# Load and first norm of a hybrid decoder step: nine row buffers, small work made between two blocks, another split of the low parts

## The chip, the cores and the metric

One core of one Trainium2 chip runs the whole program. The metric is the device time of one execution in microseconds, as the median of several executions.

## What is computed

One layer of a hybrid decoder, for 1,040 prompt tokens (16 meta tokens and 1,024 new ones) and 32 sample tokens (8 sequences of 4) over a paged cache. The part that the change touches is the beginning:

```python
def rms_norm(x, g):
    x32 = x.astype(jnp.float32)
    r = lax.rsqrt(jnp.mean(x32 * x32, axis=-1, keepdims=True) + NORM_EPS)
    return (x32 * r).astype(x.dtype) * g

def trunk_layer(x, pos, attend, conv_prev, ffn_prev, w_in, w_pa, w_pb, w_o, conv_w,
                norm1, norm2, ffn_up, ffn_conv_w, ffn_down):
    Bn, T, _ = x.shape
    hn = rms_norm(x, norm1)
    proj = hn @ w_in
    ...
    a = attend(q, k, v, qi, ki, wi)
    u, conv_new = causal_dwconv(cc * cx, conv_prev, conv_w)
    b = cb * u
    mixed = jax.nn.sigmoid(ga) * (a @ w_pa) + jax.nn.sigmoid(gb) * (b @ w_pb)
    x = x + mixed @ w_o
    hn2 = rms_norm(x, norm2)
    ...
```

Behind it come the index scores and the choice of 256 keys for each query, sparse attention, the gated short convolution, the output projection and a convolutional feed-forward with 2,816 channels. All is float32.

## The kernel before, in words

All 1,072 tokens are worked on together, features on the partitions: x is held turned, as `xt` (`core.x`), 8 feature blocks by 1,074 columns. Every product of float32 operands is made of three float32r products: high part by high part, low by high and high by low. The high part is ScalarE's copy of the operand to float32r, the low part the operand less its high part, on VectorE or POOL (GpSimd). `split_product` (L229) issues these matmuls: for each of eight feature blocks k, three column parts of 358 by three products, nine matmuls.

The program is a row of stages, each a block with a part for each engine. All engines wait for each other where one stage ends and the next begins; within a stage each engine runs its own list of instructions in the order in which it is written, held by semaphores. There is no planner; the order is the code's. Stages that matter here:

1. `load_stage` (from L295). Nine blocks of token rows, eight of 128 and one of 48, come by DMA from SP's queue into three buffers `x_rows` of 4 KB a partition (L329). Block t+3 is issued when TensorE has turned block t and ScalarE has squared it (waits in L327 and L328). For each block ScalarE sums the squares of each row (L353), TensorE turns it in eight transposes into one of three pairs of PSUM banks (L375), and VectorE copies those into `xt` (L397). When all nine are through, TensorE turns the small tables: conv weights and states (4 transposes, L380), norm gains (8, L383) and feed-forward conv weights and states (22, L386). ScalarE copies them out of PSUM (L356, L358, L360) and scales the constants ident and place (L363, L364). VectorE makes the gather rows, the cache rows that index keys are gathered from, out of the page table (L402 to L409). SP fetches the first three slices of w_in into `w_raw` (L575) and stores xt to `x_save` (L333). ScalarE's queue had issued the small tables, the constants and the page table at the start (L345 to L348).
2. `norm_stage` (from L451). VectorE and ScalarE make the inverse root of each token's mean square (`inverse_roots`, L412 on: ScalarE's `Sqrt` at L418, one Newton step on VectorE, L423 to L430). VectorE makes nine diagonal matrices of them (L504), TensorE multiplies ones by these, which spreads the numbers over the partitions (L481). For each feature block k VectorE makes `norm_y` (L508), ScalarE its high part `act_hi` (L493), and VectorE (odd k) or POOL (even k) its low part `act_lo` (L464). ScalarE and POOL also make the high and low part of the first slices of w_in (`w_hi` L546, `w_lo` L551): POOL's first ahead of its low parts, its second behind them. TensorE makes the first product, with 68 output rows, k by k as the low parts come.
3. `index_stage`. TensorE goes on with two products of 128 output rows, 72 matmuls each, on the same operands, then ropes and scores follow.

The order on POOL in the norm stage is written thus:

```python
            ahead.lo(pool, 0)
            for k in range(0, KB, 2):
                low(pool, k)
            ahead.lo(pool, 1)
```

Of the kernel before, what the change touches and what calls it, by code (L numbers as in the profile page):

```python
# [27 lines left out]
ACT = mybir.ActivationFunctionType  # L28
ALU = mybir.AluOpType
# [265 lines left out]
def load_stage(nc, core, ahead):  # L295
# [4 lines left out]
    rows = [r2(f"x_rows{s}", [128, D]) for s in range(3)]  # L300
# [7 lines left out]
    with ExitStack() as ctx:  # L308
# [3 lines left out]
        x_in = [sem(f"x_in{s}") for s in range(3)]  # L312
# [3 lines left out]
        parts = [len(x_rows(ins, t)) for t in range(NT)]  # L316
        x_count = [16 * sum(parts[t % 3:t + 1:3]) for t in range(NT)]
        ident = core.c["ident"]
        with nc.Block() as block:

            @block.sync
            def _(sp):
                sp.dma_start(core.cbuf[:, 0:128], ins["constants"][:, 0:128]).then_inc(ident_in, 16)
                for t in range(NT):
                    if t >= 3:
                        sp.wait_ge(turned, t - 2)
                        sp.wait_ge(squared, t - 2)  # L327
                    for (a, b), src in x_rows(ins, t):  # L328
                        sp.dma_start(rows[t % 3][a:b, :], src).then_inc(x_in[t % 3], 16)  # L329
# [6 lines left out]
            def _(act):  # L336
# [12 lines left out]
                act.wait_ge(ss_ok, 1)  # L349
                for t in range(NT):  # L350
                    act.wait_ge(x_in[t % 3], x_count[t])
                    after(act, squared, t)
                    act.activation(junk[0:ROWS[t], :], rows[t % 3][0:ROWS[t], :], ACT.Square,  # L353
                                   accum_out=core.ss[0:ROWS[t], t:t + 1]).then_inc(squared, 1)
                act.wait_ge(small_turned, 1)
                act.activation(core.conv[:], core.flat(6, CB * 19).rearrange("p (k r) -> p k r", r=19),  # L356
                               ACT.Copy).then_inc(small_copied, 1)
                act.activation(core.gains[:], core.flat(6, 200)[:, 100:100 + 3 * KB].rearrange("p (k r) -> p k r", r=3),  # L358
                               ACT.Copy).then_inc(small_copied, 1)
                act.activation(core.fconv[:], core.flat(7, FB * 19).rearrange("p (k r) -> p k r", r=19),  # L360
                               ACT.Copy).then_inc(small_copied, 1)
                act.wait_ge(consts_in, 16)
                act.mul(core.identb[:], core.c["ident"], -BIG)  # L363
                act.mul(core.place[:].rearrange("p s r -> p (s r)"), core.c["place"], -BIG)  # L364

            @block.tensor
            def _(pe):
                pe.wait_ge(ident_in, 16)
                for t in range(NT):
                    n = ROWS[t]  # L370
                    pe.wait_ge(x_in[t % 3], x_count[t])
# [79 lines left out]
def norm_stage(nc, core, which, name, ahead, total=None):  # L451
# [15 lines left out]
    with nc.Block() as block:  # L467
# [30 lines left out]
        def _(dve):  # L498
# [3035 lines left out]
```

## Time and profile before

| | |
|---|---|
| median of 3 runs | 1863.91 us |
| the runs | 1863.91, 1855.33, 1866.0 us |
| profiled execution, its own time | 1859.58 us |
| its span in the profile | 1857.8 us |
| granted TensorE clock, mean | 0.965 |
| TensorE busy, matmuls | 1717.0 us, 92% |
| VectorE busy | 1266.9 us, 68% |
| ScalarE busy | 682.3 us, 37% |
| POOL busy | 347.6 us, 19% |
| moved by DMA | 201.28 MB, 108 GB/s over the span |

The span is what the profiler records, first instruction to last; the execution's own time is 1.8 us longer. A timeline row names its start, its length, engine, line, operation, output and inputs, and in brackets how long the engine had been idle and what ended that. Rows of the same kind that follow each other are merged; their length is that of the whole group. "PE" is TensorE's matmuls, "PEld" its weight loads, "ACT" ScalarE, "DVE" VectorE, "ACTq" and "SPq" the queues on which DMAs are issued. The granted clock is a share of 2.4 GHz: 1.00 is 2.4, 0.50 is 1.2 GHz.

### The profile page before, as it was taken

Reading aid. Unit: us, or ns where it says so; the run is one execution under the profiler, and the core shown is the slowest. Engines: PE = TensorE matmul, PEld = TensorE weight load, DVE = VectorE, ACT = ScalarE, POOL = GpSimd, SP = SyncE. Lnnn points to the kernel's source line nnn. Section 1 sums busy time; section 2 is a strip of 40 time slices with the busy share of each in tenths; the row PEclk is TensorE's granted clock in tenths of the full one; section 3 lists DMA queues with packets and bytes.
Section 4 is the critical chain, followed back from the end, with each engine's and each line's share of the span. In section 5 each row is a group of like instructions: output and inputs, shape, how many; then the busy total and the mean of one; then the engine's idle time right before and its main releaser. Section 6 shows DMA issues by size and latency. Waiting matters only on the chain.

```text
span 1857.8 us, 30831 instructions
## 1 busy us (share of the span) xinstructions
PE 1717.0 (92%) x12025; PEld 1619.4 (87%) x12025; DVE 1266.9 (68%) x2316; ACT 682.3 (37%) x1207; POOL 347.6 (19%) x232
## 2 busy tenths in 40 slices
PE   4959999899999869988779989999999999999997
PEld 4834999899999857766569988999999999999997
DVE  4373766788888968967444268777777776664564
ACT  3253011121211245665542145333333333554453
POOL 0544143222222341222326220000000000000000
PEclk7989999999999979999989999999999999999999
DMA  8133211122222031344637312222222222776553
GB/s 263 46 93 93 57 48 39 55 67 93 78 89 64 5 110 53 134 137 136 206 116 259 105 40 88 70 77 86 81 70 73 89 71 89 257 238 201 162 180 114
DMA packets 161878, 201.28 MB, mean 108 GB/s; under 512 B 20057, under 2 KB 123449, under 8 KB 161201
## 3 DMA queue, kind: packets, MB, share of 16 engines
q1 hardware_dynamic: 142884, 125.91, 22.5%
q0 software_dynamic: 13888, 54.02, 8.7%
q10 hardware_dynamic: 4978, 19.59, 2.8%
q8 instruction: 87, 1.43, 0.3%
q14 instruction: 41, 0.34, 0.1%
HBM read 163.27 MB, written 35.61 MB: 107 GB/s over the span
## 4 chain that ended last, share of the span: by engine, by line
PE 53%; DVE 4%; ACT 3%; issue 2%; DMA 1%; POOL 0%; DVEq 0%; ACTq 0%
PE ps L2303 23%; PE ps L2708 13%; PE ps L229 7%; PE ps L1894 3%; PE ps L1938 2%; PE ps L1876 2%; PE ps L1860 1%; PE ps L1949 1%; PE ps L1975 1%; DMA down_raw<-in_ffn_down 1%; ACT probs L2082 0%; PE ps L2696 0%; DVE probs_turned L2160 0%; DVE operand_lo L3172 0%; DVE up_P_lo L3134 0%
## 5 line engine op out<-in xcount | busy, mean ns | idle before, releaser
L229 PE MATMUL ps<-act_hi,w_hi 128*128 128x358 f32 (+1 forms) x1080 | 360.9, 334 | 11.8 <-POOL act_lo L464 5.2
L2303 PE MATMUL ps<-operand_hi,up_P_hi 128*128 128x268 f32 x1232 | 354.4, 288 | 8.9 <-issue 6.8
L229 PE MATMUL ps<-act_lo,w_hi 128*128 128x358 f32 (+1 forms) x1080 | 354.7, 328 | 0.0
L229 PE MATMUL ps<-act_hi,w_lo 128*128 128x358 f32 (+1 forms) x1080 | 353.7, 328 | 0.0
L2303 PE MATMUL ps<-operand_lo,up_P_hi 128*128 128x268 f32 x1232 | 353.4, 287 | 0.0
L2303 PE MATMUL ps<-operand_hi,up_P_lo 128*128 128x268 f32 x1232 | 353.2, 287 | 0.0
L2303 PEld LDWEIGHTS ps<-operand_hi,up_P_hi 128*128 128x128 f32 x1232 | 234.0, 190 | 9.4 <-issue 7.0
L2303 PEld LDWEIGHTS ps<-operand_lo,up_P_hi 128*128 128x128 f32 x1232 | 233.6, 190 | 0.0
L2303 PEld LDWEIGHTS ps<-operand_hi,up_P_lo 128*128 128x128 f32 x1232 | 233.4, 189 | 0.0
L229 PEld LDWEIGHTS ps<-act_hi,w_hi 128*128 128x128 f32 (+1 forms) x1080 | 204.4, 189 | 14.2 <-issue 11.8
L229 PEld LDWEIGHTS ps<-act_lo,w_hi 128*128 128x128 f32 (+1 forms) x1080 | 205.0, 190 | 1.2
L229 PEld LDWEIGHTS ps<-act_hi,w_lo 128*128 128x128 f32 (+1 forms) x1080 | 203.6, 189 | 0.9
L551 POOL TENSOR_TENSOR w_lo<-w_raw,w_hi 128x1024 fp32r<-128x1024 f32 (+1 forms) x57 | 138.1, 2424 | 313.9 <-ACT w_hi L546 302.2
L2708 PE MATMUL ps<-inner_hi,down_hi 128*128 128x384 f32 (+1 forms) x528 | 172.4, 326 | 1.5 <-DVE down_lo L3295 1.5
L2708 PE MATMUL ps<-inner_hi,down_lo 128*128 128x384 f32 (+1 forms) x528 | 171.2, 324 | 0.0
L2708 PE MATMUL ps<-inner_lo,down_hi 128*128 128x384 f32 (+1 forms) x528 | 171.1, 324 | 0.0
L1102 DVE TENSOR_SCALAR_CACHE_REDUCE count_junk<-scores,candidate 128x384 uint8<-128x384 f32 (+1 forms) x186 | 163.6, 943 | 0.0
L3295 DVE TENSOR_TENSOR down_lo<-down_raw,down_hi 128x512 fp32r<-128x512 f32 x132 | 90.5, 690 | 101.4 <-ACT down_hi L2937 100.7
L2937 ACT ACTIVATE down_hi<-down_raw 128x512 fp32r<-128x512 f32 x132 | 82.6, 628 | 109.5 <-DMA down_raw<-in_ffn_down 108.9
L2816 ACT ACTIVATE up_P_hi<-w_sum 128x512 fp32r<-128x512 f32 x88 | 55.5, 632 | 170.3 <-PE ps L2303 161.7
L2708 PEld LDWEIGHTS ps<-inner_hi,down_hi 128*128 128x128 f32 x528 | 99.1, 188 | 2.4 <-DVE down_lo L3295 2.1
L2708 PEld LDWEIGHTS ps<-inner_lo,down_hi 128*128 128x128 f32 x528 | 99.1, 188 | 0.0
(421 smaller groups left out, 3114.9 us busy)
## 6 DMA issues: line engine op xcount, KB each, us to landing
down_raw<-in_ffn_down SPq DMA_DIRECT2D x132, 256.0 KB, 3.0
w_raw<-in_w_in SPq DMA_DIRECT2D x32, 512.0 KB, 3.8
w_raw<-in_ffn_up SPq DMA_DIRECT2D x48, 256.0 KB, 3.4
inner_save<-xt SPq DMA_DIRECT2D x22, 536.0 KB, 2.7
xt<-in_ffn_up SPq DMA_DIRECT2D x40, 256.0 KB, 3.3
inner_raw<-inner_save SPq DMA_DIRECT2D x44, 192.0 KB, 3.8
x_save<-xt SPq DMA_DIRECT2D x1, 4296.0 KB, 13.1
mix_b<-row ACTq DMA_DIRECT2D x8, 537.0 KB, 3.6
```

Source lines behind the costliest of these rows:

```text
L229: last = pe.matmul(core.acc(out_set)[0:rows, c, :], w(k), b(k)[:, c * CH:(c + 1) * CH], start=(i == 0 and n == 0), stop=(i == kblocks - 1 ...
L551: eng.tensor_tensor(self.core.wl[slot][:, 0:width], self.core.wr[slot][:, 0:width], self.core.wh[slot][:, 0:width].bitcast(F32), ALU.subtr ...
L1102: ins = self.dve.tensor_scalar(hd.junk[x % 2][:, 0:part.shape[1]], part, value(i), None, ALU.is_ge, ALU.add, accum_out=hd.count[:, i:i + 1])
L1860: last = pe.transpose(core.flat(4, 512, rows)[:, a:a + n], probs[2 * (s % 2) + v][0:n, 128 * k:128 * k + rows], ident[0:n, 0:n])
L1876: last = pe.matmul(core.flat(first_bank(s, v), NK[qb], n)[:, a:a + width], mine, ks[0][p, a:a + width], start=(x == 0), stop=(x == 2))
L1894: last = pe.matmul(core.flat(5, NKV * n).rearrange("p (v n) -> p v n", v=NKV), a[0:rows, k, :], b[0:rows, k, :, :], start=(k == 0 and x == 0),
L1938: last = pe.transpose(core.flat(6 + b4 % 2, 512)[:, 128 * s:128 * s + 128], got[slot][:, half(r, s)], ident)
L2303: last = pe.matmul(out[:, c, :], w[:, 128 * k:128 * k + 128], b(k)[:, cols], start=(name in OPENING and k == 0 and n == 0), stop=(k == 3 a ...
L2708: last = pe.matmul(core.ps[:, MG * (s % 2) + m, 0:w], a[:, 128 * m:128 * m + 128], c[o % H_SLOTS][:, 0:w], start=(f == 0 and z == 0), stop ...
L2816: act.activation(up_w[name][0][:], src, ACT.Copy).then_inc(w_hi, 1)
L2937: act.activation(d_hi[y][:], d_raw[y][:], ACT.Copy).then_inc(dw_hi, 1)
L3295: dve.tensor_tensor(d_lo[y][:], d_raw[y][:], d_hi[y][:].bitcast(F32), ALU.subtract).then_inc(dw_lo, 1)
```

## The change

In `load_stage`: nine buffers `x_rows`, one for each block, laid where the norm's `act_hi` and `act_lo` will stand; SP issues all of x without a wait. TensorE turns the small tables behind the fourth block (t = 3). VectorE makes the gather rows behind its copy of the fourth block. ScalarE scales ident and place and copies the small tables behind the squares of the fifth block (t = 4). Ahead of its first square it takes the root of one number.

In `norm_stage`: VectorE makes the low parts of k = 0, 2, 4, 6 and 7, POOL those of 1, 3 and 5. POOL first waits for all nine diagonals.

```diff
-    rows = [r2(f"x_rows{s}", [128, D]) for s in range(3)]
+    r1 = At(nc, Map.R1, Map.W)
+    rows = [r1(f"x_rows{t}", [128, D]) for t in range(NT)]
...
                 for t in range(NT):
-                    if t >= 3:
-                        sp.wait_ge(turned, t - 2)
-                        sp.wait_ge(squared, t - 2)
                     for (a, b), src in x_rows(ins, t):
-                        sp.dma_start(rows[t % 3][a:b, :], src).then_inc(x_in[t % 3], 16)
+                        sp.dma_start(rows[t][a:b, :], src).then_inc(x_in[t], 16)
...
                 act.wait_ge(ss_ok, 1)
+                act.wait_ge(zeroed, 1)
+                act.activation(core.root[:, 0:1], core.x[:, 0, TOK:TOK + 1], ACT.Sqrt)
                 for t in range(NT):
...
+                    if t == SMALL + 1:
+                        act.wait_ge(consts_in, 16)
+                        act.mul(core.identb[:], core.c["ident"], -BIG)
+                        act.mul(core.place[:].rearrange("p s r -> p (s r)"), core.c["place"], -BIG)
+                        act.wait_ge(small_turned, 1)
...
                     last.then_inc(turned, 1)
...
+                    if t == SMALL:
+                        turn_small()
...
                     dve.tensor_copy(core.x[:, :, 128 * t:128 * t + ROWS[t]], src[:, :, 0:ROWS[t]]).then_inc(copied, 1)
...
+                    if t == SMALL:
+                        gather_rows()
...
+    BY_DVE, BY_POOL = (0, 2, 4, 6, 7), (1, 3, 5)
...
             for k in range(KB):
                 dve.scalar_tensor_tensor(y[k][:], core.x[:, k, 0:TOK], core.gains[:, k, which:which + 1],
                                          spread_out, ALU.mult, ALU.mult).then_inc(scaled, 1)
-                if k % 2 == 0 and k:
+                if k % 2:
                     low(dve, k - 1)
             low(dve, KB - 1)
...
             pool.memset(core.al[:, :, TOK:TW].bitcast(F32), 0.0)
+            pool.wait_ge(diagonal, NT)
             ahead.lo(pool, 0)
-            for k in range(0, KB, 2):
+            for k in BY_POOL:
                 low(pool, k)
             ahead.lo(pool, 1)
```

`SMALL` is 3. `turn_small` and `gather_rows` hold the same instructions as before.

ScalarE's list from the load stage's first square to the norm's first instruction, before (`squares` is the square's throw-away output, `norm_numbers` holds sums, means and roots; L319 and the branch behind it are the change of stage):

```order
17 L353 ACTIVATE squares,norm_numbers<-x_rows_146 128x1024
18 L353 ACTIVATE squares,norm_numbers<-x_rows_147 48x1024
19 L356 ACTIVATE conv_w_and_states<-ps 128x76
20 L358 ACTIVATE gains<-ps 128x24
21 L360 ACTIVATE ffn_conv_w_and_states<-ps 128x418
22 L363 ACTIVATE ident_bf_55<-constants 128x128
23 L364 ACTIVATE place_bf_54<-constants 128x256
24 L319 UNCONDITIONAL_BRANCH
25 L487 UNCONDITIONAL_BRANCH
26 L418 ACT_TABLE_LOAD
27 L418 ACTIVATE norm_numbers<-norm_numbers 128x9
```

and in the changed kernel:

```order
15 L353 ACTIVATE squares,norm_numbers<-x_rows_149 128x1024
16 L357 ACTIVATE ident_bf_55<-constants 128x128
17 L358 ACTIVATE place_bf_54<-constants 128x256
18 L360 ACTIVATE conv_w_and_states<-ps 128x76
19 L362 ACTIVATE gains<-ps 128x24
20 L364 ACTIVATE ffn_conv_w_and_states<-ps 128x418
21 L353 ACTIVATE squares,norm_numbers<-x_rows_150 128x1024
22 L353 ACTIVATE squares,norm_numbers<-x_rows_151 128x1024
23 L353 ACTIVATE squares,norm_numbers<-x_rows_152 128x1024
24 L353 ACTIVATE squares,norm_numbers<-x_rows_153 48x1024
25 L320 UNCONDITIONAL_BRANCH
26 L501 UNCONDITIONAL_BRANCH
```

Five instructions went from behind the last square to behind the fifth, and the table load ahead of the norm's root is gone.

VectorE's list in the norm stage, from the first y on, before:

```order
17 L508 SCALAR_TENSOR_TENSOR norm_y_402<-xt,gains,ps 128x1072
18 L508 SCALAR_TENSOR_TENSOR norm_y_403<-xt,gains,ps 128x1072
19 L508 SCALAR_TENSOR_TENSOR norm_y_404<-xt,gains,ps 128x1072
20 L464 TENSOR_TENSOR act_lo<-norm_y_403,act_hi 128x1072
21 L508 SCALAR_TENSOR_TENSOR norm_y_405<-xt,gains,ps 128x1072
22 L508 SCALAR_TENSOR_TENSOR norm_y_406<-xt,gains,ps 128x1072
23 L464 TENSOR_TENSOR act_lo<-norm_y_405,act_hi 128x1072
```

and in the changed kernel, where `norm_y_398` is the first:

```order
18 L522 SCALAR_TENSOR_TENSOR norm_y_398<-xt,gains,ps 128x1072
19 L522 SCALAR_TENSOR_TENSOR norm_y_399<-xt,gains,ps 128x1072
20 L472 TENSOR_TENSOR act_lo<-norm_y_398,act_hi 128x1072
21 L522 SCALAR_TENSOR_TENSOR norm_y_400<-xt,gains,ps 128x1072
22 L522 SCALAR_TENSOR_TENSOR norm_y_401<-xt,gains,ps 128x1072
23 L472 TENSOR_TENSOR act_lo<-norm_y_400,act_hi 128x1072
```

The first low part now stands behind the second y and is VectorE's.

POOL's list in the changed kernel's norm stage:

```order
9 L566 TENSOR_TENSOR w_lo_68<-w_raw_62,w_hi_65 128x544
10 L472 TENSOR_TENSOR act_lo<-norm_y_399,act_hi 128x1072
11 L472 TENSOR_TENSOR act_lo<-norm_y_401,act_hi 128x1072
12 L472 TENSOR_TENSOR act_lo<-norm_y_403,act_hi 128x1072
13 L566 TENSOR_TENSOR w_lo_69<-w_raw_63,w_hi_66 128x1024
```

Before, four low parts stood there (k = 0, 2, 4, 6); now three (k = 1, 3, 5).

## Rows read from the trace of the kernel before

**Rows 1.** The page: the span, and each engine's busy time
```profile
span 1857.8 us, 30831 instructions
...
PE 1717.0 (92%) x12025; PEld 1619.4 (87%) x12025; DVE 1266.9 (68%) x2316; ACT 682.3 (37%) x1207; POOL 347.6 (19%) x232
```

**Rows 2.** Busy time by stretch: length, engines, then granted clock, DMA share, GB/s
```profile
16.00:18.00 2.00, 1.51 (x7) 1.51 (x8) 1.21 (x1) 1.40 (x3) 0.00 (x0) 1.00 0.43 113
...
22.00:24.00 2.00, 1.09 (x8) 0.86 (x8) 0.26 (x1) 1.14 (x2) 0.00 (x0) 1.00 0.93 294
...
26.00:28.00 2.00, 2.00 (x13) 1.67 (x12) 0.48 (x1) 1.91 (x4) 0.00 (x0) 0.50 1.23 278
...
52.00:54.00 2.00, 2.00 (x10) 1.62 (x9) 2.00 (x2) 1.35 (x2) 1.40 (x1) 0.72 0.00 0
...
54.00:56.00 2.00, 2.00 (x15) 1.68 (x14) 2.00 (x2) 2.00 (x3) 1.14 (x1) 1.00 0.00 0
...
62.50:86.50 24.00, 23.95 (x146) 23.76 (x146) 0.00 (x0) 3.20 (x4) 6.55 (x3) 1.00 0.32 79
```

**Rows 3.** Timeline of the load stage: start us, us, engine, line, operation
```profile
16.49 3.17 PE L375 MATMUL ps<-constants,x_rows 128*128 128x128 f32 x16 [0.55 <-DMA x_rows<-in_x_prompt]
...
19.90 1.10 PE L375 MATMUL ps<-constants,x_rows 128*128 128x128 f32 x8 [0.24 <-DMA x_rows<-in_x_prompt]
...
26.86 1.06 ACT L353 ACTIVATE squares<-x_rows 48x1024 f32<-48x1024 f32 x1
...
27.52 1.69 DVE L397 COPY xt<-ps 128x1024 f32<-128x1024 f32 x2 [2.28 <-PE ps L375]
...
29.73 2.51 PE L386 MATMUL ps<-constants,ffn_conv_rows 19*128 19x19 f32 x22
32.28 0.23 ACT L356 ACTIVATE conv_w_and_states<-ps 128x76 f32<-128x76 f32 x1 [4.26 <-PE ps L386]
...
33.08 0.43 ACT L364 ACTIVATE place_bf<-constants 128x256 bf16<-128x256 f32 x1
```

**Rows 4.** DMA issues of 0 to 60 us: median us from issue to landing
```profile
x_rows<-in_x_prompt SPq DMA_DIRECT2D x7, 512.0 KB, 5.3
constants<-in_constants ACTq DMA_DIRECT2D x1, 1561.0 KB, 11.6
...
pages<-in_page_table ACTq DMA_DIRECT2D x1, 128.0 KB, 12.8
```

**Rows 5.** Timeline of the norm stage up to the spreading products
```profile
33.76 1.28 ACT L418 ACT_TABLE_LOAD   x1 [0.26 <-PEq L319]
...
35.90 1.33 POOL L551 TENSOR_TENSOR w_lo<-w_raw,w_hi 128x544 fp32r<-128x544 f32 x1 [1.98 <-ACT w_hi L546]
35.95 1.29 DVE L430 SCALAR_TENSOR_TENSOR norm_numbers<-norm_numbers 128x9 f32<-128x9 f32 x1
37.28 1.85 DVE L504 TENSOR_SCALAR norm_diagonals<-constants,norm_numbers 128x128 f32<-128x128 f32 x9
...
37.62 4.37 PE L481 MATMUL ps<-norm_diagonals,constants 128*128 128x128 f32 x18 [5.38 <-DVE norm_diagonals L504]
```

**Rows 6.** Timeline from the first y to the next stage's first matmul
```profile
42.03 3.81 DVE L508 SCALAR_TENSOR_TENSOR norm_y<-xt,gains,ps 128x1072 f32<-128x1072 f32 x3 [2.90 <-PE ps L481]
...
44.56 5.99 POOL L464 TENSOR_TENSOR act_lo<-norm_y,act_hi 128x1072 fp32r<-128x1072 f32 x2 [7.34 <-ACT act_hi L493]
45.76 2.45 DVE L464 TENSOR_TENSOR act_lo<-norm_y,act_hi 128x1072 fp32r<-128x1072 f32 x1
...
47.22 0.54 PE L229 MATMUL ps<-act_hi,w_hi 128*68 128x358 f32 x1 [5.23 <-POOL act_lo L464]
...
58.68 1.28 DVE L464 TENSOR_TENSOR act_lo<-norm_y,act_hi 128x1072 fp32r<-128x1072 f32 x1 [1.17 <-ACT act_hi L493]
...
58.76 3.44 POOL L551 TENSOR_TENSOR w_lo<-w_raw,w_hi 128x1024 fp32r<-128x1024 f32 x1
...
62.55 0.41 PE L229 MATMUL ps<-act_hi,w_hi 128*128 128x358 f32 x1 [0.54 <-PEq L467]
```

More of the change, by code:

```diff
@@ L315, in load_stage @@
         ins = core.i
-        parts = [len(x_rows(ins, t)) for t in range(NT)]
-        x_count = [16 * sum(parts[t % 3:t + 1:3]) for t in range(NT)]
+        x_count = [16 * len(x_rows(ins, t)) for t in range(NT)]
+        SMALL = 3
         ident = core.c["ident"]
@@ L360, in _ @@
[L360 to L364, printed above, removed]
+                    if t == SMALL + 1:
[3 more added lines that the diff above has]
+                        act.wait_ge(small_turned, 1)
+                        act.activation(core.conv[:], core.flat(6, CB * 19).rearrange("p (k r) -> p k r", r=19),
+                                       ACT.Copy).then_inc(small_copied, 1)
+                        act.activation(core.gains[:], core.flat(6, 200)[:, 100:100 + 3 * KB].rearrange("p (k r) -> p k r", r=3),
+                                       ACT.Copy).then_inc(small_copied, 1)
+                        act.activation(core.fconv[:], core.flat(7, FB * 19).rearrange("p (k r) -> p k r", r=19),
+                                       ACT.Copy).then_inc(small_copied, 1)
@@ L393, in _, with gather_rows @@
                 dve.memset(core.x[:, :, TOK:TW], 0.0).then_inc(zeroed, 1)
+                def gather_rows():
+                    dve.wait_ge(pages_in, 16)
+                    dve.wait_ge(consts_in, 16)
+                    dve.tensor_tensor(picked[:].rearrange("p (m q) -> p m q", q=PPG),
+                                      pages[:].rearrange("p (m q) -> p m q", q=PPG),
+                                      core.c["page"].rearrange("p (m q) -> p m q", m=1).broadcast_to([128, NB * NGA, PPG]),
+                                      ALU.mult).then_inc(own, 1)
+                    dve.wait_ge(own, 1)
+                    dve.tensor_reduce(page[:], picked[:].rearrange("p (m q) -> p m q", q=PPG), AX.X, ALU.add).then_inc(own, 1)
+                    dve.wait_ge(own, 2)
+                    dve.tensor_scalar(core.rows[:], page[:], float(PAGE // RUN), core.c["lane"], ALU.mult, ALU.add)
                 for t in range(NT):
@@ L464, in low, with lows @@
         eng.tensor_tensor(core.al[:, k, 0:TOK], y[k][:], core.ah[:, k, 0:TOK].bitcast(F32), ALU.subtract)\
-            .then_inc(lo_odd if k % 2 else lo_even, 1)
+            .then_inc(lo_p if k in BY_POOL else lo_d, 1)
+    def lows(pe, k):
+        if k in BY_POOL:
+            pe.wait_ge(lo_p, BY_POOL.index(k) + 1)
+        else:
+            pe.wait_ge(lo_d, BY_DVE.index(k) + 1)
     with nc.Block() as block:
@@ L484, in _ @@
             ahead.w.product(pe, 0, 0, 0, m=ahead.m,
-                            before=lambda k: pe.wait_ge(lo_odd if k % 2 else lo_even, k // 2 + 1)).then_inc(ahead.ready, 1)
+                            before=lambda k: lows(pe, k)).then_inc(ahead.ready, 1)
         @block.scalar
```

50 lines of the change are left out of this document (18 added, 32 removed).

## The prediction

> **What bounds the kernel now.** I read the page first, for the shares; then busy time and granted clock in short stretches of the first 90 us, where the change lies; then the timeline there, engine by engine; last the DMA issues. TensorE is busy for 1717 of 1857.8 us [rows 1], so after its first long product the kernel hangs on that engine, and a block of time taken out ahead of that product moves all that follows, unchanged, by as much. That only holds because nothing later waits for something that doesn't move along: x_save, the weights and the gathers are issued on signals of the same stages.
>
> In the first 90 us it is different. From 62.5 to 86.5 us TensorE is busy 23.95 of 24 us [rows 2]. Before that it isn't the bound. The load stage hands over at 33.76 us, where ScalarE starts on the norm [rows 5]. Read backwards: the last thing ended there is ScalarE's copy for place (33.08 and 0.43), which follows the three small copies from 32.28 us on, and these idled 4.26 us for TensorE's small transposes, 34 of them, the last 22 in 2.51 us [rows 3], 0.114 us each. So the tail is: x copied at 29.21 (27.52 and 1.69), ScalarE's last square done at 28.02, and yet 4.5 us pass until the stage ends.
>
> The norm then goes in a chain: table for the root 1.28, root, four small steps on VectorE of which the last took 1.29 instead of about 0.17, nine diagonals 1.85, nine spreading products 4.37 [rows 5]. The first y starts at 42.03. From there VectorE, ScalarE and POOL share the rows; the first product starts at 47.22 and the next stage's first at 62.55 [rows 6], which is 20.52 us behind the first y.
>
> **The load stage.** Small transposes, three copies, two scalings and the gather rows are moved from behind the ninth block to behind the fourth or fifth. Nothing is added there but one root of one number, done while ScalarE would wait for x in any case.
>
> The transfers: three buffers made x late. In 16 to 18 us the DMA engines were busy 0.43 of the time with 113 GB/s, in 22 to 24 us 0.93 at 294 GB/s [rows 2], so some 316 GB/s were there for x alone. Left after about 16.5 us are blocks 5 to 8, 3 x 512 KB and 192 KB, 1.77 MB: 5.6 us at that rate, so the last lands at about 22.5 us instead of 26.8. Constants and page table need 11.6 and 12.8 us to land [rows 4], so at 15.6 and 17.3; the deeper SP queue was never empty before 16 us anyway, so I leave both where they are. The weights come behind x on the same queue, 1.33 MB, at some 27 us, and are wanted later.
>
> TensorE: the fourth and fifth block took 3.17 us from 16.49 on, 1.58 each; the sixth 1.10 [rows 3]. The small ones therefore start at 18.1. At the old 0.114 us they end at 22.0; the sixth block's pace, 0.7 of its forerunners', would make it 20.8; between the two I take 21.5. Then VectorE copies blocks 4 to 8: it needs 1.25 a block and 0.55 for the last (1.69 for a whole and a short one, with their overlap), so if TensorE turns a block in 1.10, copies run from 22.6 to 28.2. If it turns one in 1.58 throughout, from 22.0: 4 x 1.58 and about 1.0 for the short block, then the short copy, 29.9. ScalarE: five squares by 19.0, scalings 0.75, waits for the small transposes, copies 0.75, then four squares at 1.25: done at 27.5 to 28. Gather rows, 1.1 us, fill VectorE's wait for the fifth block. With x_save's issue of 0.35 and the hand-over (0.25 behind ScalarE's last end in rows 3 and 5) the stage ends at 28.8 or 30.5, and I take 29.1, nearer to the first since the sixth block's pace held already at 19.9 us. **Gain 4.7 us**, 3.3 to 5.4.
>
> **Ahead of y.** The table load of 1.28 at 33.76 goes, for the Sqrt table, loaded in front, serves Square and Copy too: there is no second load in the instruction order. VectorE's last small step ran 35.95 to 37.24 and POOL's w_lo 35.90 to 37.23 [rows 5]: it stood still until POOL ended. POOL now waits for all nine diagonals, so 1.12 us go. What is queued behind POOL's new wait is w_lo and its first low part; the diagonals end about 3.2 us into the stage, w_lo (1.33) at 4.6, and the product wants it at 10. Gain 2.4; less 0.2 for semaphores, **2.2 us**.
> The Trainium skill (ScalarE: Activation LUTs, What ACT_TABLE_LOAD costs) prices a switch of sets at 1283 ns for the load plus 1380 ns of drain, 2.66 us in all; this trace agrees with the first only, since the root started 1.29 us after its load. By the page the sum would be 1.4 us better.
>
> **The low parts.** One takes VectorE 1.28 (58.68) and POOL 2.4 (two of them 5.99, less 1.28 in which VectorE went between). The two stand in each other's way: VectorE's low part of 45.76 took 2.45, ending 1.28 after POOL's first had ended, and POOL's w_lo of 58.76 took 3.44 beside VectorE's [rows 6]. The y steps read one operand from PSUM and don't wait. With these rules I laid out the new order, in us from the first y. VectorE: y0, y1, low 0 at 2.5, y2, y3, low 2 at 6.3, y4, y5, low 4 at 10.1, y6, y7 until 13.85, low 6, low 7. POOL: low 1 at 3.8, low 3 at 7.6, low 5 at 11.4 until 13.85, w_lo. Here low 6 and w_lo want the same port at once, and whoever comes second waits; in either order, with POOL's w_lo at 2.4, low 7 ends at about 18.9. TensorE starts at 3.9 instead of 5.2, but is held at low 7 and has nine matmuls left, 9 x 0.166 [rows 2]: end 20.4, hand-over 20.8 against 20.52. **Loss 0.3 us**, from a gain of 1.3 (were only the early start to count) to a loss of 1.5.
> The Trainium skill (SBUF — State Buffer, Who interferes with whom) says that a VectorE instruction with two SBUF inputs and a POOL instruction that reads SBUF exclude each other for a whole instruction, the first issued winning. The rows of 45.76 and 58.76 agree. If VectorE could go on beside POOL, the new order would end low 7 at 16.4, TensorE would be held by nothing but its own 14.8 us, and the sum be 1.7 us better.
>
> **Sum.** 4.7 + 2.2 - 0.3 = 6.6 us. Against the profiled execution, 1859.58, that is 1853.0. The runs shown are 1855.33, 1863.91 and 1866.0; the profiled one lies 4.3 under their median. The mean of all four is 1861.2, and 6.6 off it gives **1854.6**, my forecast. About 0.5%, 9.3 us, is what a measurement of this kernel tells from no change, so the likeliest result is no change that can be told, on the faster side.
>
> **Rivals.**
> (a) The deeper queue brings x no sooner: the last block still lands at 26.8. For it: in the first 16 us the DMA engines were full in any case, and transfers of 512 KB took 5.3 us each [rows 4]. Against: the idle share at 16 to 18 us. Copies then end at 29.2 as now, and with the small work out of the tail the stage ends at 29.8: gain 4.0 + 2.2 - 0.3 = 5.9, 1855.3. Chance 0.15.
> (b) The clock is at 2.4 GHz where it was at 1.2. The granted clock was 0.50 from about 26 to 53 us [rows 2], over the spreading products and the first third of the first product. TensorE now has fewer rests between 16 and 28 us. If the nine spreading products take half of 4.37, y starts 2.2 us sooner, and transposes at the better pace save another 0.6: gain 9.4, and 1851.8. Against: it worked without rest from 25.6 to 32.2 us and stayed at 0.50. Chance 0.2.
> (c) VectorE and POOL collide more often than laid out, by one POOL low part, 2.4 us: low 4 and low 6 each come within 0.1 us of a POOL instruction. Gain 4.2, 1857.0. Chance 0.1.
> (d) **Slower.** The hold at low 6 or low 7, up to 1.8 us, and the hand-over right behind it let the clock fall to 1.2 GHz, and the next stage's 144 matmuls run at about 0.30 us instead of 0.166 (in the first product 5.9 us at half clock went for some 19). It decides from 6.6 / 0.134 = 49 matmuls on; with all 144 the change costs 19.3 - 6.6 = 12.7 us, 1873.9. For it: once at 0.50, the clock stayed there for 27 us. Against: before, TensorE rested 2.1 us ahead of 22.9 and the clock was still 1.00 in 22 to 24. Chance 0.05.
> The Trainium skill (TensorE: Matmul & The Clock Gate, Why this matters for your kernels) has the rests between bursts of matmuls throw the engine back to the half rate, which is the mechanism of (d); no row here shows it at a rest as short as 1.8 us.
>
> **Numbers.** Forecast 0.5, (a) 0.15, (b) 0.2, (c) 0.1, (d) 0.05. All but (d) lie between gains of 4.2 and 9.4; the four runs of before scatter by 4 to 5 us around their mean, and their medians by less. So 1847.5 to 1861.0 leaves out (d) and the ends of the scatter. Faster by over 0.5%: most of (b), three in ten of the forecast, a little of (a), together 0.33; slower 0.05 for (d); 0.62 between.
>
> **What would show it.** The norm's first instruction at 28.5 to 30.8 us instead of 33.76; squares without a table load between root and load; the diagonals starting 1.4 us into the norm instead of 3.5; y0 6.1 us into it; the next stage's first matmul 20.8 us behind y0, with a hold of 1 to 2 us ahead of the seventh or eighth row; x landed by 23 us. The prediction is wrong if the stage still ends beyond 31 us, if the clock is under 1.00 after 60 us where it wasn't, or if the time between the index stage's first matmul and the end isn't the same 1795 us within 3.

## The result, and the profile after

| | kernel before | changed kernel |
|---|---|---|
| median of 20 runs each | 1863.74 us | 1856.38 us |
| range of the runs | 1855.33 to 1868.98 | 1851.46 to 1861.92 |
| ratio of the times | 1 | 0.9969 [0.9961, 0.9978] |

The medians lie 7.4 us apart; the ratio says 5.8 us less (4.1 to 7.3): within 0.5%, on the faster side. The forecast was 1854.6, 6.6 us less. Below stand the same four points of the two profiled executions. "Forecast" is the gain that the prediction gave to the step.

| us from the span's start | before | changed | gain of the step | forecast |
|---|---|---|---|---|
| the norm's first instruction | 33.76 | 30.69 | 3.07 | 4.7 |
| first y | 42.03, 8.27 later | 36.41, 5.72 later | 2.55 | 2.2 |
| next stage's first matmul | 62.55, 20.52 later | 56.66, 20.25 later | 0.27 | -0.3 |
| end of the span | 1795.3 later | 1797.8 later | -2.5 | 0 |

The first three steps give 5.89 us and the last takes 2.5 back, so the spans differ by 3.4. The 2.5 isn't to be read as a price of the change: the profiled execution of the kernel before, 1859.58, lies 4.2 us under that kernel's median, the changed one's, 1856.2, at its own. TensorE's busy time is what it was [rows 1], as the page of the changed kernel shows.

```profile
span 1854.4 us, 30826 instructions
...
PE 1719.0 (93%) x12025; PEld 1620.5 (87%) x12025; DVE 1267.3 (68%) x2317; ACT 681.3 (37%) x1207; POOL 340.9 (18%) x231
```

**The load stage.** The timeline of the changed kernel's load stage (start us, us, engine, line, operation, idle before):

```profile
7.14 16.19 SPq L590 DMA_DIRECT2D w_raw<-in_w_in  x3
...
14.29 1.09 PE L389 MATMUL ps<-constants,x_rows 128*128 128x128 f32 x8 [2.49 <-DMA x_rows<-in_x_prompt]
...
16.60 1.97 PE L389 MATMUL ps<-constants,x_rows 128*128 128x128 f32 x8 [1.22 <-DMA x_rows<-in_x_prompt]
...
19.80 2.51 PE L378 MATMUL ps<-constants,ffn_conv_rows 19*128 19x19 f32 x22
...
22.24 6.08 PE L389 MATMUL ps<-constants,x_rows 128*128 128x128 f32 x40
...
25.95 3.95 DVE L414 COPY xt<-ps 128x1024 f32<-128x1024 f32 x4 [0.48 <-PE ps L389]
...
29.93 0.35 SPq L331 DMA_DIRECT2D x_save<-xt  x1
30.69 0.11 POOL L530 MEMSET act_hi<- 128x16 f32 x1 [30.23 <-POOLq L320]
```

Here TensorE never waits for x again after 16.60: the fourth block, the small transposes from 18.50 and the last five blocks follow on each other to 28.3, and the copies end at 29.90 behind them. All the small work stands in that unbroken chain. Two paces can be told apart: transposes of a whole block start 0.11 us apart at the quick one and 0.21 at the slow one, the small ones 0.06 and 0.11. Busy time of the same kernel by stretch (length, engines, then granted clock, DMA share, GB/s) and one row of its DMA issues (the last is the time from issue to landing in us) say what the transfers and the clock did:

```profile
16.00:18.00 2.00, 1.40 (x7) 1.40 (x8) 0.65 (x1) 1.19 (x3) 0.00 (x0) 0.50 1.04 412
...
20.00:22.00 2.00, 2.00 (x21) 2.00 (x21) 0.82 (x3) 0.00 (x0) 0.00 (x0) 0.50 1.17 214
22.00:24.00 2.00, 2.00 (x11) 1.96 (x11) 0.00 (x0) 1.65 (x5) 0.00 (x0) 0.50 1.27 233
24.00:26.00 2.00, 2.00 (x11) 2.00 (x11) 1.27 (x2) 1.82 (x5) 0.00 (x0) 0.54 1.21 289
26.00:28.00 2.00, 2.00 (x22) 1.83 (x21) 2.00 (x2) 1.74 (x4) 0.00 (x0) 1.00 0.44 108
...
x_rows<-in_x_sample SPq DMA_DIRECT2D x1, 128.0 KB, 17.3
```

The transfers ran at 412 GB/s in 16 to 18 us where 113 stood before [rows 2], but only at 214 and 233 in 20 to 24 us, and constants and page table had their part of it. The last piece of x, issued at 6.68, landed 17.3 us later, at 24.0. The kernel before had it at 26.4; my forecast was about 22.5. The rate was as forecast: from the landing of the fourth block at 16.6 on, five blocks, 2.29 MB, came in 7.4 us, 310 GB/s against my 316. But I had taken the fifth block as landed by then, and ScalarE waited for it until 17.96. Nothing hung on that: TensorE came to the last block at 27.6. But the clock was at its lower level, 1.2 GHz, from about 16 to 26 us. In 24 to 26 us TensorE does 11 transposes in 2 us, in 26 to 28 us, at 2.4 GHz, 22 (six of them of the last, short block).

**Ahead of y, and the low parts.** The same timeline from the norm's start:

```profile
30.94 0.21 ACT L425 ACTIVATE norm_numbers<-norm_numbers 128x9 f32<-128x9 f32 x1 [3.11 <-DVE norm_numbers L428]
...
31.83 0.17 DVE L437 SCALAR_TENSOR_TENSOR norm_numbers<-norm_numbers 128x9 f32<-128x9 f32 x1
32.03 1.85 DVE L518 TENSOR_SCALAR norm_diagonals<-constants,norm_numbers 128x128 f32<-128x128 f32 x9
32.38 3.99 PE L495 MATMUL ps<-norm_diagonals,constants 128*128 128x128 f32 x18 [4.06 <-DVE norm_diagonals L518]
33.97 1.33 POOL L566 TENSOR_TENSOR w_lo<-w_raw,w_hi 128x544 fp32r<-128x544 f32 x1 [3.12 <-DVE norm_diagonals L518]
...
40.32 0.54 PE L229 MATMUL ps<-act_hi,w_hi 128*68 128x358 f32 x1 [3.95 <-DVE act_lo L472]
...
43.87 2.08 POOL L472 TENSOR_TENSOR act_lo<-norm_y,act_hi 128x1072 fp32r<-128x1072 f32 x1 [1.60 <-ACT act_hi L507]
...
49.61 2.40 POOL L566 TENSOR_TENSOR w_lo<-w_raw,w_hi 128x1024 fp32r<-128x1024 f32 x1
...
49.95 4.37 DVE L472 TENSOR_TENSOR act_lo<-norm_y,act_hi 128x1072 fp32r<-128x1072 f32 x2
...
53.20 0.38 PE L229 MATMUL ps<-act_hi,w_hi 128*68 128x358 f32 x1 [1.15 <-DVE act_lo L472]
```

No table is loaded, the last small step takes 0.17 instead of 1.29 [rows 5], the diagonals start 1.34 us into the norm instead of 3.52, and w_lo follows them. In the low parts, POOL's (k = 1, 3, 5) take 2.08 to 2.10 each. Before, the two with VectorE's between them took 5.99 [rows 6], and the two that met no low part of VectorE took 2.54 and 2.51, so it isn't VectorE alone that made them longer:

```profile
56.29 2.51 POOL L464 TENSOR_TENSOR act_lo<-norm_y,act_hi 128x1072 fp32r<-128x1072 f32 x1 [1.15 <-ACT act_hi L493]
```

That row is of the kernel before, k = 6; VectorE made its last y until 57.51 and then stood idle to 58.68. Whether it is the even k, or what the other engines do beside it in the old split, that makes 2.5 us of 2.1 stays open.

The last two low parts of VectorE take 4.37 together beside POOL's w_lo. TensorE is held for the first of them: 1.15 us ahead of the seventh row (k = 6), with the 18 matmuls of the last two rows still to come, 0.163 us apart. For low 7, which ends at 54.32, 17.9 behind the first y, it isn't held.

### The profile page after: what moved, and what is told of

Its sections match the earlier page's. It is cut to its first block, busy times and chain, and to the rows that moved or that the text cites. A ratio compares the mean times of both kernels' runs of the same rounds, so it can differ in the third digit from the quotient of the medians.

```text
span 1854.4 us, 30826 instructions
## 1 busy us (share of the span) xinstructions
PE 1719.0 (93%) x12025; PEld 1620.5 (87%) x12025; DVE 1267.3 (68%) x2317; ACT 681.3 (37%) x1207; POOL 340.9 (18%) x231
## 4 chain that ended last, share of the span: by engine, by line
PE 53%; DVE 4%; ACT 3%; issue 2%; DMA 1%; POOL 0%; DVEq 0%; ACTq 0%
PE ps L2318 23%; PE ps L2723 13%; PE ps L229 7%; PE ps L1909 3%; PE ps L1953 2%; PE ps L1891 2%; PE ps L1875 1%; PE ps L1964 1%; PE ps L1990 1%; DMA down_raw<-in_ffn_down 1%; ACT probs L2097 0%; PE ps L2711 0%; DVE probs_turned L2175 0%; DVE operand_lo L3187 0%; DVE up_P_lo L3149 0%
```

## Experiments

Theory A is the one that I held when I wrote the expectation, B its rival. "Rest" is the time from the next stage's first matmul to the end of the span. All edits are against the changed kernel.

**1. Is it the buffers or the place of the small work?** Nine buffers, the small work back behind the last block (this, the same for VectorE's gather rows, and `t == SMALL + 1` on ScalarE likewise):

```
-                    if t == SMALL:
+                    if t == NT - 1:
```

> The changed kernel with its nine buffers, but the small transposes, their copies, the scalings and the gather rows stand behind the ninth block again. Theory A (from the fourth block on TensorE never rests, so its sum of work sets the end wherever the small transposes stand, and only the tail behind them differs): TensorE's last small transpose ends at about 28.5 us, ScalarE's three copies 0.75 later, and the norm starts at 29.5 us, about 1.2 us before the changed kernel's 30.69. Theory B (it is taking the small work out of the tail that gave the 3 us, as the prediction had it for most of its 4.7): the norm starts 2.5 to 4 us later than 30.69, at 33.2 to 34.7 us. What follows the norm's start keeps its 5.7 us to the first y and 25.9 us to the next stage's first matmul within 0.5, in both.

Measured, median of nine executions: 1853.68 us (1851.36 to 1860.01), ratio 0.9951 [0.9935, 0.9966]. The norm starts at 27.75, against 30.69 with the small work mid-load. The timeline of TensorE:

```profile
16.31 5.64 PE L389 MATMUL ps<-constants,x_rows 128*128 128x128 f32 x32 [0.23 <-DMA x_rows<-in_x_prompt]
...
22.71 1.80 PE L389 MATMUL ps<-constants,x_rows 128*128 128x128 f32 x16 [0.75 <-DMA x_rows<-in_x_prompt]
...
25.20 1.51 PE L378 MATMUL ps<-constants,ffn_conv_rows 19*128 19x19 f32 x22
```

Theory A is right that the norm comes no later; it comes sooner by more than A said (29.5). The last two blocks wait for x, so x is the bound to 22.7, and the small transposes take 1.51 where they took 2.51. Against 33.76 the stage comes 6.0 us sooner without the new place. About 0.5 of that is the order on ScalarE: the two scalings stand ahead of its wait for the small transposes here, and stood behind the small copies before (to 33.51). Part is the clock: the transposes turn quick at 20.3 here, and stay so over all the small work, so this run alone doesn't settle how much. The times don't settle it either, since the intervals of the two ratios, [0.9935, 0.9966] and [0.9961, 0.9978], meet.

**2. The place without the buffers.** Three buffers with their waits on SP as before, the small work mid-load.

```
-    rows = [r1(f"x_rows{t}", [128, D]) for t in range(NT)]
+    rows = [r1(f"x_rows{t}", [128, D]) for t in range(3)] * 3
...
+                    if t >= 3:
+                        sp.wait_ge(turned, t - 2)
+                        sp.wait_ge(squared, t - 2)
```

> The changed kernel with three row buffers again and SP's waits for them; the small work stays behind the fourth block. Theory A (the nine buffers let x land before TensorE wants it, and three would now be worse than before since each fetch waits for a turned block that stands behind 3.7 us of small transposes): the last blocks land at 28 to 30 us and the norm starts at 32 to 34 us. Theory B (rival (a) of the prediction: the DMA engines were full anyway and the buffers brought nothing): the norm starts within 0.7 us of the changed kernel's 30.69.

Measured, a single execution: 1855.44 us; norm 31.43, between the two ranges. The timeline shows the last two blocks waiting for x:

```profile
21.76 4.72 PE L393 MATMUL ps<-constants,x_rows 128*128 128x128 f32 x24
...
27.39 1.09 PE L393 MATMUL ps<-constants,x_rows 128*128 128x128 f32 x8 [0.91 <-DMA x_rows<-in_x_prompt]
...
29.36 0.69 PE L393 MATMUL ps<-constants,x_rows 48*128 48x48 f32 x8 [0.89 <-DMA x_rows<-in_x_sample]
```

With three buffers x is the bound to the last block; with nine it is TensorE. Beside the changed kernel's 30.69 the buffers' worth is small, 0.74 us. And against 33.76 the small work's place alone is worth 2.3 us, as long as there are three buffers. All of these are single profiles.

**3. The old split of the low parts**, with the wait for the diagonals kept.

```
-    BY_DVE, BY_POOL = (0, 2, 4, 6, 7), (1, 3, 5)
+    BY_DVE, BY_POOL = (1, 3, 5, 7), (0, 2, 4, 6)
```

> The changed kernel with the old split of the low parts (POOL k = 0, 2, 4, 6, VectorE 1, 3, 5, 7), the wait for the diagonals kept. Norm start 30.7 and first y 36.4 us unchanged. Theory A (the new split starts the product 1.3 us sooner and gives it back at the collision of low 6 with POOL's w_lo): next stage's first matmul 20.3 to 20.8 us behind the first y, against 20.25 in the changed kernel. Theory B (the early start is what counts): 21.5 us or more behind the first y.

Measured, a single execution: 1860.84 us. The next stage's first matmul comes 20.48 behind the first y, as before the change (20.52), against 20.25. The timeline has the old collisions again:

```profile
39.51 5.98 POOL L472 TENSOR_TENSOR act_lo<-norm_y,act_hi 128x1072 fp32r<-128x1072 f32 x2 [4.02 <-ACT act_hi L507]
40.71 2.42 DVE L472 TENSOR_TENSOR act_lo<-norm_y,act_hi 128x1072 fp32r<-128x1072 f32 x1
```

The split is worth 0.23 us, a gain where I had a loss of 0.3. The time of 1860.84 says little about it, since the rest took 1801.6 here.

**4. Without POOL's wait for the diagonals** (the line `pool.wait_ge(diagonal, NT)` taken out).

> The changed kernel without POOL's wait for the nine diagonals. Theory A (POOL's w_lo holds the port that VectorE's small steps and diagonals want): one of VectorE's small steps or the diagonals stands still until w_lo, 1.33 us, ends, and the first y comes 0.8 to 1.4 us later than 5.72 us behind the norm's start. Theory B (with the table load gone, the chain on VectorE is ahead of w_lo and they don't meet, or the spreading products hide it): the first y stays within 0.2 us.

Measured, a single execution: 1853.56 us. The timeline around the small steps:

```profile
29.01 1.32 POOL L565 TENSOR_TENSOR w_lo<-w_raw,w_hi 128x544 fp32r<-128x544 f32 x1 [0.93 <-ACT w_hi L560]
29.07 1.29 DVE L437 SCALAR_TENSOR_TENSOR norm_numbers<-norm_numbers 128x9 f32<-128x9 f32 x1
30.40 1.85 DVE L518 TENSOR_SCALAR norm_diagonals<-constants,norm_numbers 128x128 f32<-128x128 f32 x9
```

VectorE stands still until POOL ends, 1.29 instead of 0.17, and the diagonals start 2.48 into the norm instead of 1.34. The 1.12 us of the forecast are right: it is 1.14. The Trainium skill (SBUF — State Buffer, Who interferes with whom) says that a VectorE instruction with two inputs in SBUF and a POOL instruction that reads SBUF exclude each other for a whole instruction; this run agrees, with 1.29 against 0.17.

The load stage held a surprise. Its code is that of the changed kernel to the letter, but the norm starts at 27.92, not 30.69:

```profile
16.05 1.59 PE L389 MATMUL ps<-constants,x_rows 128*128 128x128 f32 x8 [0.53 <-DMA x_rows<-in_x_prompt]
...
18.33 1.52 PE L378 MATMUL ps<-constants,ffn_conv_rows 19*128 19x19 f32 x22
19.78 6.00 PE L389 MATMUL ps<-constants,x_rows 128*128 128x128 f32 x40
```

The small transposes take 1.52 instead of 2.51 and the last five blocks start 2.46 us sooner, 0.55 of it since x came sooner. The other 1.9 us are TensorE's pace. In the changed kernel's profile it had the quick one at the third block (14.29, 1.09) and had lost it by 16 us; here it has it from the fourth block to about 20.5, over just the small work.

**5. POOL's last w_lo behind VectorE's last low part.**

```
+            pool.wait_ge(lo_d, len(BY_DVE))
```

> The changed kernel, but POOL's second w_lo waits until VectorE has made all five of its low parts. Theory A (low 6 and low 7 stood still for w_lo, and that hold set the end of the first product): low 6 and low 7 take 2.5 us together instead of 4.37, the hold ahead of the seventh row goes, and the next stage's first matmul comes 18.7 to 19.3 us behind the first y instead of 20.25; w_lo ends before TensorE does. Theory B (the hold is covered, or w_lo, now last, holds the next stage up instead): 20.0 us or more behind the first y.

Measured, median of nine executions: 1854.9 us (1851.12 to 1860.37), ratio 0.9953 [0.9936, 0.997]. The next stage's first matmul comes 18.87 behind the first y, 1.38 less. The timeline:

```profile
50.78 0.38 PE L229 MATMUL ps<-act_hi,w_hi 128*68 128x358 f32 x1 [0.34 <-POOL act_lo L472]
...
51.03 2.52 DVE L472 TENSOR_TENSOR act_lo<-norm_y,act_hi 128x1072 fp32r<-128x1072 f32 x2
...
53.63 2.38 POOL L567 TENSOR_TENSOR w_lo<-w_raw,w_hi 128x1024 fp32r<-128x1024 f32 x1 [2.91 <-DVE act_lo L472]
```

The pair of low parts goes from 4.37 to 2.52, and the hold of 1.15 ahead of the seventh row is gone; what is left is 0.34 ahead of the sixth, for POOL's low part. So that collision was the price of the new split. One part of theory A fails: w_lo doesn't end before TensorE does. The first product ends at 55.51, w_lo at 56.01, and the next stage starts behind w_lo, so of the 1.9 us that the product gains 0.5 go again.

**6. The small work behind the second block** instead of the fourth.

```
-                    if t == SMALL:
+                    if t == 1:
```

> The changed kernel with TensorE's 34 small transposes behind the second block of x instead of the fourth; ScalarE's and VectorE's work stays where it is. Theory A (behind the second block TensorE waits 2.5 us for x anyway, behind the fourth it has no rest, so the small work is only free there): x blocks 4 to 8 are turned without a gap from about 18 us at full clock or 20 at half, and the norm starts 1 to 2.5 us earlier than the same kernel would at the same clock, that is 26.5 to 29 us. Theory B (only the sum of work counts, or the small tables land too late for this place): the norm starts at 27.9 (full clock) to 30.7 us (half clock), as it did in two runs of this load stage.

Measured, median of four executions: 1852.79 us (1851.11 to 1857.1), ratio 0.9936 [0.9915, 0.9957]. The norm starts at 27.11. The timeline, and the clock of one stretch of it:

```profile
12.90 2.51 PE L378 MATMUL ps<-constants,ffn_conv_rows 19*128 19x19 f32 x22
15.34 6.80 PE L389 MATMUL ps<-constants,x_rows 128*128 128x128 f32 x40
...
22.82 1.71 PE L389 MATMUL ps<-constants,x_rows 128*128 128x128 f32 x16 [0.67 <-DMA x_rows<-in_x_prompt]
...
13.00:14.00 1.00, 1.00 (x12) 1.00 (x11) 0.00 (x0) 0.14 (x1) 0.00 (x0) 1.00 1.08 448
```

The small ones go at the slow pace here too, and it costs nothing: they fill the time in which TensorE waited for the third block anyway (2.49 us at 14.29 in the changed kernel), and the last two blocks wait for x again. Its ratio's interval lies clear of the changed kernel's [0.9961, 0.9978]. The window's clock reads 1.00 at the slow pace. So ahead of its first fall the clock column doesn't tell the pace; durations do. In the kernel before it is the same: the column has 1.00 at 16 to 18 us [rows 2], and the blocks of 16.49 were turned at the slow pace until 18.9.

**7. Without the root ahead of the load** (its two lines on ScalarE taken out).

> The changed kernel without the root of one number ahead of the squares. Theory A (the table load then stands ahead of the norm's root again, 1.28 us on the path, while nothing is added in the load stage): the first y comes 1.0 to 1.3 us later behind the norm's start, 6.7 to 7.4 us instead of 5.7 to 6.1. Theory B (the page's account of a switch, with its drain): 2.4 us or more later.

Measured, a single execution: 1858.15 us. The timeline:

```profile
30.57 1.28 ACT L423 ACT_TABLE_LOAD   x1 [3.43 <-PEq L320]
31.86 0.21 ACT L423 ACTIVATE norm_numbers<-norm_numbers 128x9 f32<-128x9 f32 x1
```

The diagonals start 2.39 into the norm instead of 1.34: the load is worth 1.05 us, since 0.25 of it lies where the root waited for VectorE's first step. The Trainium skill (ScalarE: Activation LUTs, What ACT_TABLE_LOAD costs) puts 1380 ns of drain on top of the load. The measurement decides against that on this path: the root starts 1.29 after its load starts. ScalarE had been idle for 3.43 us ahead of the load, so what a load costs right behind running work isn't shown.

**8. Does work for TensorE between the first blocks keep the clock up?** Nine products of the identity ahead of the first block and eight ahead of the third, into a part of PSUM that is free.

```
+                    for _ in range({0: 9, 2: 8}.get(t, 0)):
+                        pe.matmul(core.flat(7, 128), ident, ident, start=True, stop=True)
```

> The changed kernel with TensorE multiplying ident by ident into a bank not yet in use, nine times ahead of the first block of x and eight times behind the second, where it waits for x anyway (this adds work that no output needs). Theory A (what the load stage lost against my forecast is the clock at 1.2 GHz in the small transposes and blocks 3 to 7, and a busier TensorE gets the higher level): the granted clock is 1.00 between 12 and 24 us, the last 22 small transposes take about 1.5 us instead of 2.51, and the norm starts at 27 to 28 us. Theory B (the clock falls in this stretch all the same, or the fillers push the blocks back): small transposes at 2.5 us and a norm start of 30 us or more.

Measured, a single execution: 1857.09 us; norm 29.93, just under theory B's 30.

```profile
10.35 1.09 PE L391 MATMUL ps<-constants,x_rows 128*128 128x128 f32 x8 [0.96 <-DMA x_rows<-in_x_prompt]
...
18.88 2.46 PE L378 MATMUL ps<-constants,ffn_conv_rows 19*128 19x19 f32 x22
21.27 6.52 PE L391 MATMUL ps<-constants,x_rows 128*128 128x128 f32 x40
...
51.94 0.38 PE L229 MATMUL ps<-act_hi,w_hi 128*68 128x358 f32 x1 [1.80 <-DVE act_lo L474]
...
54.00:55.00 1.00, 1.00 (x5) 0.75 (x4) 0.00 (x0) 0.00 (x0) 0.00 (x0) 0.50 0.00 0
```

The quick pace came earlier, at the second block, but was gone in the small work all the same; the clock was 0.50 from 20 to 24 us. The fillers left rests of 1.38 and 1.40 us ahead of the third and fourth block, so a TensorE without rests wasn't tried.

Further on something came that no other run has. The next stage's first matmul came 21.81 behind the first y, 1.56 later than in the changed kernel. TensorE was held for 1.80 us ahead of the seventh row; at 53.1 us the clock fell to 0.50, and eleven of the last matmuls started 0.30 apart instead of 0.163. That is the mechanism of rival (d), at a smaller price, since the clock was back with the next stage. A hold alone doesn't do it: holds of 1.76 to 1.79 at the same place left the clock at 1.00 in experiments 1, 2 and 6. What fell together here wasn't found.

**9 to 11. The changed kernel once more, and two mixtures**, on one chip with the same executions of the kernel before (median 1861.87 us of 18). `both` is experiments 5 and 6 together, `last_and_w_lo` 1 and 5.

> The changed kernel once more, as the measure for the two beside it on the same chip. The norm starts at 27.9 to 31.4 us, by the clock in the load stage; the next stage's first matmul comes 25.9 us behind that; the time is 0.9955 to 0.998 of the kernel before.

> The changed kernel with both edits that gained on their own: small transposes behind the second block of x, and POOL's second w_lo behind VectorE's last low part. Theory A (the two gains lie in different stages on the same path and add): the norm starts at 26.5 to 29 us, the next stage's first matmul 24.6 us behind it, so 51 to 54 us, and the time is 2 to 4.5 us under that of the changed kernel beside it. Theory B (what follows, with its clock at 1.2 GHz here and there between 100 and 155 us, gives the gain back): the next stage's first matmul as said, but the time within 1 us of the changed kernel's.

> The changed kernel with its nine buffers, the small work behind the ninth block, as before, and POOL's second w_lo behind VectorE's last low part. Theory A (moving the small work from the end to behind the fourth block brought nothing): norm start 27.8 us at full clock to 29.5 at half, next stage's first matmul 24.6 us behind it, and 1 to 3 us less time than the changed kernel beside it. Theory B (the small work's place is worth its 3 to 4 us, and the one run that said otherwise owed it to the clock): norm start at 31 us or more in a profile at half clock, and the time no better than the changed kernel's.

| | median us | ratio | norm's first | behind first y | rest |
|---|---|---|---|---|---|
| changed_again | 1857.58 | 0.9973 [0.9962, 0.9985] | 29.70 | 20.28 | 1800.7 |
| last_and_w_lo | 1852.64 | 0.9949 [0.9931, 0.9967] | 29.14 | 18.87 | 1796.7 |
| both | 1849.34 | 0.9935 [0.9916, 0.9955] | 26.67 | 18.88 | 1795.3 |

The medians are of 12, 7 and 6 executions, and "behind first y" is the next stage's first matmul. `both` beats both kernels: its median lies 12.5 us under the kernel before and 8.2 under the changed one. I had expected 2 to 4.5 under the changed one, and for `last_and_w_lo` 1 to 3 where 4.9 came. In the profiles the early start explains 4.0 and 1.5 of these; the remainder lies in the rest and has no explanation here. The next stage of `both` starts at 51.65, 10.9 us sooner than before. The last wait ahead of it is that of experiment 5, for the w_lo that was put last:

```profile
48.91 2.38 POOL L567 TENSOR_TENSOR w_lo<-w_raw,w_hi 128x1024 fp32r<-128x1024 f32 x1 [2.89 <-DVE act_lo L472]
...
51.65 0.41 PE L229 MATMUL ps<-act_hi,w_hi 128*128 128x358 f32 x1 [0.84 <-PEq L481]
```

**What the load profiles say together.** With nine buffers and the small work mid-load, six profiles have the norm's first instruction at 27.92, 29.70, 30.57, 30.69, 30.87 and 31.39: mean 30.2. With the small work last there are 27.75 and 29.14, with it behind the second block 26.67 and 27.11. So against 33.76 the whole change gives about 3.6 us in this stage (2.4 to 5.8), nine buffers with the small work left last 4.6 to 6.0, the early place 6.7 to 7.1, and the changed kernel's place with three buffers 2.3. The 33.76 is one profile too, and its own scatter isn't known.

**The rest of the span.** It took 1795.3 us before, 1797.8 in the changed kernel's profile and 1800.7 in its second one, with the same instructions; over the other ten kernels 1795.3 to 1801.8, in no order that follows the edits. The busy time of 670 to 930 us, of before, changed_again and both:

```profile
670.00:930.00 260.00, 215.32 (x1952) 167.25 (x1954) 189.28 (x395) 147.94 (x326) 67.75 (x68) 0.94 0.41 136
```
```profile
670.00:930.00 260.00, 217.34 (x1966) 170.50 (x1966) 184.58 (x393) 147.15 (x326) 63.17 (x65) 0.92 0.41 136
```
```profile
670.00:930.00 260.00, 220.07 (x2066) 172.02 (x2067) 184.46 (x400) 151.47 (x343) 63.17 (x65) 0.94 0.41 136
```

The executions with the longest rests, 1800.5 to 1801.8, have 0.91 or 0.92 here (changed_again, small_early, u_small_last, u_old_split), the two with 1795.3 have 0.94, and those between 0.93, the changed kernel's profile too. Two hundredths of the mean are 260 x 0.02 / 0.5 = 10 us more at half clock, which could account for up to 5 us. Rest and clock go together over all thirteen profiles; but no run changed the clock alone, so it isn't shown as the cause. What lets the clock fall in one execution and not in another wasn't found, and whether an earlier start of the stages makes it likelier stays open: `both` starts earliest and has the shortest rest.

## Why the prediction was right, and where it wasn't

**Time and likeliest case: right.** 1856.38 against 1854.6, inside the range, within 0.5% on the faster side. But the sizes were off, and luck had its part: the load stage gave 1.6 us less than forecast, the other two steps 0.9 more. The 0.5% that I took for what can be told from no change was too coarse; the interval of 20 executions each leaves 1 out by far.

**The load stage, 4.7 us: mis-sized.** It measured 3.07, under the lower bound of 3.3, and 3.6 as the mean of six profiles. The step that failed is the choice between two paces: "if TensorE turns a block in 1.10" the copies end at 28.2, "if it turns one in 1.58 throughout" at 29.9, and I took 29.1 for the norm since the sixth block's pace held at 19.9 us. They ended at 29.90: the slow branch. In the kernel before the quick pace lay over 19.0 to 25.8 us, in the changed one over 14.3 to 15.6 and from 25.8 on, and I carried it over to a stage that the change itself had rearranged. (The hand-over took 0.79 where I had 0.60.) The chain was right in kind: small transposes from 18.1, here 18.50, then five blocks without a wait for x. What I never worked out is the same stage with nine buffers and the small work left last. I took the gain for that of the shorter tail, for 4.0 of the 4.7 by rival (a)'s sum; experiment 2 has 2.3 for it, with three buffers. And with x landing sooner TensorE had little left to wait for behind the fourth block, 0.75 us in experiment 1 and 1.45 in `last_and_w_lo`, so that the work put there made its own chain longer. The free place is behind the second block, where the wait remains (experiment 6). That x landed 1.5 us later than forecast, a block short in my sum, had no effect.

**Ahead of y, 2.2 us: right.** Experiments 7 and 4 give 1.05 for the table and 1.14 for the standing still, 2.19 in sum. The profile's 2.55 has 0.38 more from nine spreading products that took 3.99 instead of 4.37; in changed kernels with 4.37 the first y comes 6.10 behind, a gain of 2.17.

**The low parts, -0.3: wrong sign, and the last step wrong.** +0.27 in the profile, 0.23 in experiment 3. TensorE starts 3.91 behind the first y, as said (3.9); low 6 and w_lo collide, as said. But I had TensorE "held at low 7" with nine matmuls left, and it was held at low 6 with eighteen left: low 6 ended at 53.1, and 18 x 0.163 behind it make the product's end, while low 7 was through before its row came. Low 7 ended 17.9 behind the first y and not 18.9. POOL's low part, 2.4 by my division of two collided ones, took 2.1 in the new split; w_lo ended 15.6 behind the first y and not 16.3, and low 7 2.3 behind that. Experiment 5 shows the collision's own price, 1.38, net of the 0.5 that w_lo then costs.

**The rivals.** (a) fell: the last of x landed at 24.0, 2.4 us sooner than before. (b) happened in part, and by the execution: experiment 4 had the quick pace over the small work and gained 2.8 more. (c) didn't happen, POOL's low parts stayed at 2.08 to 2.10. (d) didn't come in the changed kernel: a hold of 1.15 left the clock at 1.00, with products 0.163 us apart behind it. But it isn't impossible: in experiment 8 the clock fell behind a hold of 1.80, for 1.6 us and not 19.

Of the signs that I had named, x missed: it had landed by 24.0 us and not by 23.

**"The same 1795 us within 3": held once, failed once.** 1797.8 in the first profile, 1800.7 in the second. The 1795 was the rest of one execution, and one of the shorter: at the median time of 1863.74 and the same start it would be some 4 us more. So the change needn't have lengthened anything. It fits that 6.9 us of earlier start (62.55 to 55.62) came to 4.3 in the medians of experiment 9 and to 5.8 in the first ratio.

## What to carry to other kernels

Two edits that aim at the same wait aren't to be added up: once the deeper queue had taken the wait for x away, the work moved into it was in the way, and two blocks earlier, in a wait that the queue doesn't touch, it was free. So work out each edit alone as well as all together. Where two engines share a way to memory, look which instruction of the slower engine can go last; a single wait was worth 1.4 us here, a whole new split 0.2. And an expected gain under the scatter of single executions, some 6 us in this kernel, is read at the stage's own instructions in the timeline, not from the end of the span.

## What the runs showed of the hardware that I had not expected

- The same load code took 27.92 to 31.39 us in six executions. The place of TensorE's quick spell differs: over the third block at 14.29 in one, over the small work at 18.33 in another (2.51 and 1.52 us for the same 22 transposes).
- The clock column reads 1.00 from the start until its first fall, even where the transposes have the slow pace (experiment 6).
- POOL's subtraction of 128x1072 took 2.08 to 2.11 us for k = 1, 3 and 5, and 2.49 to 2.54 for the even k of the old split (before, experiment 3) even where VectorE made none beside it. VectorE's took 1.27 or 1.28 for either.
- SP's three issues of the weights took 16.19 us with nine buffers, with nine blocks of x queued ahead of them, and held nobody: x_save was wanted at 29.93, and the issues ended at 23.33.
- With products of the identity in part of TensorE's rests the clock fell in the load stage nevertheless (experiment 8), and once more behind a hold of 1.80 us, where three other executions with such a hold kept it.
